# Last layer's end of an expert-mixture kernel: order of two sums and three norms, and the queue that stores the outputs

## What is computed

```python
def rms_norm(x, g):
    y = x * lax.rsqrt(jnp.mean(x * x, axis=-1, keepdims=True) + EPS)
    return y * g
...
    return x + m[5] * y                     # end of the expert mixture: y is its sum over experts
...
y_prompt = rms_norm(xc, final_norm_g)       # (1, 128, 1024)
y_sample = rms_norm(xs, final_norm_g)       # (1, 256, 1024)
```

## Time and profile before

| what | value |
|---|---|
| median of 3 runs | 1044.03 us (1043.95 to 1044.31) |
| the profiled execution's own time | 1044.46 us |
| its span in the trace | 1042.3 us |
| PE busy | 932.8 us, 89% |
| DVE busy | 462.1 us, 44% |
| ACT busy | 226.7 us, 22% |
| POOL busy | 106.9 us, 10% |

### The profile page before, as it was taken

How to read it: one execution, slowest core, us unless ns; L and a number is a source line. 1 busy time by engine, 2 the same in 40 slices (tenths; PEclk the granted TensorE clock), 3 DMA queues, 4 the chain that set the end, 5 groups by cost and what they waited for, 6 DMA issues and landing times.

```text
span 1042.3 us, 11963 instructions
## 1 busy us (share of the span) xinstructions
PE 932.8 (89%) x4160; PEld 469.1 (45%) x4160; DVE 462.1 (44%) x1035; ACT 226.7 (22%) x460; POOL 106.9 (10%) x165
## 2 busy tenths in 40 slices
PE   2799999999989999999988997899799999999980
PEld 0455454645343444444433465445444444545430
DVE  1157633244433444444554365624334444444454
ACT  2223132212211211211222114311111112111111
POOL 2300011300210000000001101020010000000002
PEclk9899999899989999999998999999699999999995
DMA  9992350947899999999996543021599999999921
GB/s 304 362 348 81 123 182 30 373 157 288 333 366 420 420 421 420 419 421 421 415 379 245 183 161 132 0 87 41 204 419 419 420 420 421 421 420 419 416 83 60
DMA packets 76135, 303.59 MB, mean 291 GB/s; under 512 B 9593, under 2 KB 9905, under 8 KB 50632
## 3 DMA queue, kind: packets, MB, share of 16 engines
q1 hardware_dynamic: 66504, 281.28, 68.1%
q0 software_dynamic: 8320, 17.18, 4.9%
q10 hardware_dynamic: 1280, 4.72, 1.2%
HBM read 309.75 MB, written 5.32 MB: 302 GB/s over the span
## 4 chain that ended last, share of the span: by engine, by line
PE 70%; DMA 15%; DVE 6%; issue 3%; ACT 3%; SPq 2%; POOL 0%; POOLq 0%; DVEq 0%; ACTq 0%
PE psum L1024 17%; PE psum L705 16%; DMA ring<-in_w_exp_up 11%; PE psum L1050 7%; PE psum L777 4%; PE psum L903 4%; PE psum L729 4%; PE psum L998 2%; DVE ht L1797 2%; DMA ring<-in_w_mod 2%; DMA arena<-h_rows,arena 2%; PE psum L1012 2%; PE psum L1013 1%; PE psum L978 1%; PE psum L951 1%
## 5 line engine op out<-in xcount | busy, mean ns | idle before, releaser
L1024 PE MATMUL psum<-ring,arena 128*64 128x512 f32 x1024 | 226.7, 594 | 8.4 <-DMA ring<-in_w_exp_up 6.6
L705 PE MATMUL psum<-ring,ht 128*128 128x512 f32 (+1 forms) x432 | 170.5, 552 | 3.4 <-ACT ht L1225 2.7
L1024 PEld LDWEIGHTS psum<-ring,arena 128*64 128x64 f32 x1024 | 85.1, 137 | 146.6 <-issue 142.0
L1050 PE MATMUL psum<-ring,arena 128*64 128x512 f32 x512 | 116.9, 599 | 8.3 <-DVE ht L1797 7.2
L705 PEld LDWEIGHTS psum<-ring,ht 128*128 128x128 f32 x432 | 81.5, 192 | 85.7 <-issue 77.3
L1797 DVE TENSOR_TENSOR ht<-ht,psum 128x512 f32<-128x512 f32 x172 | 105.5, 682 | 4.1 <-PE psum L1013 2.0
L1840 DVE TENSOR_TENSOR arena<-arena,psum 128x256 f32<-128x256 f32 x32 | 13.5, 422 | 172.5 <-ACT arena L1368 172.5
L1375 ACT ACTIVATE y_top<-psum,arena 128x512 fp32r<-128x512 f32 x64 | 44.0, 687 | 183.7 <-PE psum L1050 183.7
L1012 PE MATMUL psum<-y_top,to_token 128*128 128x512 f32 x192 | 80.3, 418 | 3.5 <-DVE y_low L1828 3.5
L1828 DVE SCALAR_TENSOR_TENSOR y_low<-psum,arena,y_top 128x512 fp32r<-128x512 f32 x64 | 48.0, 751 | 79.2 <-ACT y_top L1375 79.2
L1013 PE MATMUL psum<-y_low,to_token 128*128 128x512 f32 x192 | 76.9, 401 | 0.0
(11 more groups left out here) (301 smaller groups left out, 899.5 us busy)
## 6 DMA issues: line engine op xcount, KB each, us to landing
ring<-in_w_exp_gate SPq DMA_DIRECT2D x32, 2048.0 KB, 18.0
ring<-in_w_exp_up SPq DMA_DIRECT2D x32, 2048.0 KB, 23.0
ring<-in_w_exp_down SPq DMA_DIRECT2D x32, 2048.0 KB, 20.5
ring<-in_w_mod SPq DMA_DIRECT2D x24, 2048.0 KB, 15.1
ring<-in_w_in_even SPq DMA_DIRECT2D x5, 2048.0 KB, 19.9
ring<-in_w_in_odd SPq DMA_DIRECT2D x3, 2048.0 KB, 19.6
ring<-in_w_out_even SPq DMA_DIRECT2D x2, 2048.0 KB, 8.5
shift_scale<-mod_rows POOLq DMA_DIRECT2D x2, 2048.0 KB, 10.1
```

The source lines that it names most:

```text
L705: mm = pe.matmul(psum[:, to, 0:cols], HT[:, b, k, :], w[:, k, :], start=(k == 0), stop=(k == KC - 1))
L1024: mm = pe.matmul(psum[64 * e:64 * e + 64, 2, :], XT[:, k, 64 * e:64 * e + 64], RG[:, 3 * v:3 * v + 2, e, k, :], start=(k == 0), stop=(k == ...
L1050: mm = pe.matmul(psum[64 * e:64 * e + 64, 4 + n, :], HTS[v][:, k, 64 * e:64 * e + 64], RD[:, 3 * v + 2, e, k, n * 512:(n + 1) * 512], star ...
```

## The change

VectorE: in the last layer (l = 1) gated_sum(2) comes ahead of norm_block(4, 0), so that both sums stand in a row and the three norms follow in a row. In the first layer the order stays. The final scaling L1489 is made in two halves of 512 columns, each with its own increment of h_ready. The stores of the outputs leave POOL's list; SP issues them instead behind its weight loads, one for each half of each block (six of 256 KB), and SP waits for them at its end.

```diff
@@ SP, behind experts(1) @@
             experts(1, lambda slot: used_up(sp, last_in(slot, len(CHUNKS))))
+            for b in range(NB):
+                dst = outs["y_prompt"][0] if b == 0 else outs["y_sample"][0, (b - 1) * P:b * P]
+                for n in range(2):
+                    cols = slice(n * 512, (n + 1) * 512)
+                    sp.wait_ge(S("h_ready"), 2 * NB * 4 + 2 * b + n + 1)
+                    sp.dma_start(dst[:, cols], H[:, b, cols]).then_inc(S("h_stored"), 16)
+            sp.wait_ge(S("h_stored"), 16 * NB * 2 + 16 * 2 * NB)
@@ POOL, behind experts(1) @@
-            for b in range(NB):
-                pool.wait_ge(S("h_ready"), 2 * NB * 4 + b + 1)
-                dst = outs["y_prompt"][0] if b == 0 else outs["y_sample"][0, (b - 1) * P:b * P]
-                pool.dma_start(dst, H[:, b, :]).then_inc(S("stored"), 16)
-            pool.wait_ge(S("stored"), 16 * 9)
@@ VectorE, norm_apply @@
                 if u == 4:
-                    dve.scalar_tensor_tensor(H[:, b, :], X[:, b, :], root, GS[:, 0, 0, :], ALU.mult, ALU.mult).then_inc(S("h_ready"), 1)
+                    for n in range(2):
+                        cols = slice(n * 512, (n + 1) * 512)
+                        dve.scalar_tensor_tensor(H[:, b, cols], X[:, b, cols], root, GS[:, 0, 0, cols], ALU.mult, ALU.mult).then_inc(S("h_ready"), 1)
                     return
@@ VectorE, end of experts(l) @@
                 gated_sum(1)
-                norm_block(u + 1, 0)
-                gated_sum(2)
+                if l == 0:
+                    norm_block(u + 1, 0)
+                    gated_sum(2)
+                else:
+                    gated_sum(2)
+                    norm_block(u + 1, 0)
                 norm_block(u + 1, 1)
                 norm_block(u + 1, 2)
```

## The result

| | before | after |
|---|---|---|
| median of 5 runs | 1044.03 us (1043.75 to 1044.31) | 1032.09 us (1030.93 to 1034.35) |
| ratio after to before | | 0.9892, 95% interval 0.9879 to 0.9906 |
| the profiled execution | 1044.46 us | 1034.35 us |
| its span | 1042.3 us | 1032.2 us |

The change makes the kernel 1.1% faster. 1034.0 us was forecast, with 1032.9 to 1035.8 as the range. The profiled execution came out where its sum had put it (1034.35 against 1034.5, and 1032.2 against 1032.3 of span). That both meet so closely is partly luck: the part ahead of the change took 1013.41 us here and 1013.34 before, while over four traces of the changed kernel it lies anywhere from 1010.8 to 1015.8, as the experiments show.

The account below looks back on a forecast made before the run. The end was taken as VectorE's serial chain, then POOL's store and drain. Savings of 8.8 us drain, 0.3 VectorE and 0.9 store make 10.0: 1044.46 to 1034.5, less 0.43 for the median, 1034.0 us; range 1032.9 to 1035.8.

Parts of the forecast that it names:

- The large term: Program's end: POOL's drain, taken as 8.7 us, moves from behind the last store to beside VectorE's work, saving 8.8 us.
- The link L1464: Small VectorE instruction in each norm, old L1462: one stall beside POOL's adds near 0.83 us, two free at 0.16.
- two halves: VectorE's final scaling per block: 1.41 us to the last end, 1.33 to the next start, so +0.13 a block.
- adds covered: POOL's adds behind VectorE's sums: tighter buffer slack is 0.58 us, so following closely costs nothing.
- The wake: SP's delay from the ready last half to its store's issue: bounds 0 to 0.3 us, taken as 0.15.
- Landing: SP's last half-block store, from issue to landing: 2.0 to 2.3 us, taken as 2.1, upper bound 2.9.
- The end of SP: Program's end on SP, after the last landing, its short drain and the engines' meeting: forecast at 1032.34 us.
- The tail that follows the last store: Program's end: the empty stretch follows the last store whoever issues it; time 1042.8 us, chance 0.07.
- The drain kept off by VectorE: Program's end: VectorE's scalings hold up POOL's drain until 1029.7 us; time 1040.4 us, chance 0.05.
- VectorE kept off by the drain: Norms at the end: POOL's drain blocks VectorE, moving all by 8.8 us; time 1042.8 us, chance 0.04.
- The price per store: Program's end: a queue's drain pays 2.91 us per store, so SP pays 17.4 us for six; time 1051.5, chance 0.04.

Follow-up runs that it names:

- two chains: Changed kernel with block 2's adds moved from POOL to VectorE and the roots of blocks 0 and 1 made together on two columns; 1032.28 us, ratio 0.9886.
- Queue only: Changed kernel with the old order of sums and norms, keeping SP's stores in halves; 1035.91 us, ratio 0.9909 to the kernel before.
- POOL waits too: Changed kernel with POOL also waiting for all six of SP's stores to land before it ends; 1041.38 us, ratio 0.9964 to the kernel before.
- the early table: Two chains plus an unread ScalarE root right behind block 0's squares, to load the table earlier; 1032.4 us, ratio 0.9908 to the kernel before.

## Why the prediction was right, and where it was wrong

**The large term was right.** 8.8 us were to come from POOL's drain going beside VectorE's work. With a wait of POOL for the last landing put back, 8.5 us return. Its length was the unknown: 8.725 with three stores ahead of it, 8.48 with none, about 8.5 from the end of the last add in the others. What POOL does in it no trace shows.

**VectorE.** Last half forecast at 1029.66, found at 1029.72 with a first update 0.07 later. The link L1464 took 0.83 once and 0.16 twice, two halves took 1.41, adds covered: all as worked out. The Trainium skill's lock (SBUF — State Buffer, "SBUF: two separate sides") agrees with every trace here: a two-input instruction that starts 0.8 us before the end of one of POOL's adds is held to that end (0.83 against 0.16), and in two chains, where no POOL add is left by then, no such stall is seen. An instruction in the last 0.1 us of an add is not held: L1472 at 1021.38 took its 0.15, though POOL's third add ends near 1021.5 (1017.58 and three quarters of 5.23).

**SP.** The wake was 0.15 in the sum; the last issue comes within 0.1 of the ready half. Landing was 2.1, measured 2.0. The end of SP was forecast at 1032.34 and the span is 1032.2.

**The split between the parts was not seen.** The prediction named the order as worth 0.3 us on VectorE's chain, and did not say that without it the drain would run 1.9 us past SP (1034.5 against 1032.6). Queue only shows it: order and queue have to come together for the last 2.5 us.

**The rivals.** The tail that follows the last store: out, by 0.2 us between SP's drain and the end of the span. The rule of the Trainium skill that stood behind it (VectorE: DVE Perf Modes, "The DRAIN you can't avoid"), about 12 ns on all five engines, holds for SP (13 ns) and not for POOL (8.48 us with nothing in flight); here the measurement decides. The drain kept off by VectorE: out, 9.81 us in the changed kernel and in queue only alike, with VectorE busy. VectorE kept off by the drain: out, L1465 at 1022.86 took 0.16. The price per store: out, by POOL waits too.

**The step that failed** is the last one, "the median before is 0.43 below the profiled execution, so 1034.0 us", together with a range whose ends were made only of terms of the end. It took for granted that what lies ahead of the end takes equally long in each execution, because three times lay within 0.4 us. In 61 further runs the kernel before spread over 12 us (1038.22 to 1050.11), and in its traces and those of the changed kernel the first update starts anywhere from 1010.8 to 1015.8 us. The forecast was right for the difference and too narrow for the number: the four traces of the changed kernel have ends of 18.79 to 18.83, the two of the kernel before 28.88 and 28.96, a difference of 10.1 where 10.0 was forecast. The 1.9 us by which the first median lies below it are within the spread of five runs, and in three further comparisons the ratios were 0.9893, 0.9902 and 0.9904, at or a little below 0.9904, which 10.0 of 1044 us make. Whether the change does anything upstream at all is bounded by that, at about 2 us either way, and no more closely. Two ratios of the variants sit at the edge of their intervals, in opposite directions: POOL waits too has an end only 1.7 us shorter than before, where its times say 2.0 to 5.5, and the early table one that is 12.2 shorter, where its times say 7.0 to 12.2. Neither is explained; the lengths inside the traces carry the argument, not the times.

## What to carry to other kernels

Look at what follows the last store: a stretch without any work in it belongs to some engine, and the drain rows say to which. An engine whose drain is long should be the first to finish, so take its last waits and stores away, and then order the others' work so that its last real instruction comes early. Measure such a change by a length inside the trace that leaves the noisy part out, and set a range for the total time by the spread of many runs, not of three.

## What the runs showed of the hardware that was not expected

POOL's drain at the program's end takes 8.48 us with nothing in flight, and VectorE's and DMA's work beside it neither lengthens it (8.5 us from the last add's end) nor is slowed by it (0.16 us for a link of the root, 2.0 us for a store's landing, with and without the drain). Whether its length depends on the software DMAs earlier in the kernel was not tried; every kernel here has them. About 10 us of TensorE at 1.2 GHz between 640 and 660 us go with 2.6 us between two executions of the same kernel, while from 743 to 1013 us all twelve traces agree within 0.4 us (270.25 to 270.56 from the first load to the first update). There the DMA engines are always busy (417 GB/s from 743 to 980 us in the changed kernel's first trace); that this is why the clock does not show there was not tested. And ScalarE's table load of 1.28 us, hidden until then, came onto the path by moving one root behind one more pair of squares, and left it with an early root that nobody reads.
